# One filler object through the recurrence and the attention, its first weights split earlier, the recurrence's preparation cut into parts, and its stores issued by ACT

## The reference

```python
def in_proj(xn, w_in, b_fgate, lb):                 # xn: (1, 2048, 1024); w_in: (1024, 8200)
    h = xn @ w_in
    fq, fk, fv, ff, fz, hq, hf, hi, hz, mq, mz, ga, gb, gm = split(h)
    f = lb + (1.0 - lb) * sigmoid(hf)               # hg_k = 1 - f, hg_logf = log(f)
    ...
def fox_prompt(q, k, v, logf):                      # 8 heads x 64, causal
    sc = q @ k.T * scale + c[:, None] - c[None, :]  # c = cumsum(logf)
    return softmax(sc) @ v
def hgrn2(q, k, v, logf, s0, chunk):                # 4 heads x 128, over chunks of rows
    b = cumsum(logf)
    o = (q . exp(b[t] - b[s]) . k) @ v + (q * exp(b)) @ S
    S = exp(b[-1]) * S + (k * exp(b[-1] - b)).T @ v
def merge_branches(...):
    mixed = sigmoid(ga) * ya + sigmoid(gb) * yb + sigmoid(gm) * ym
    return x + mixed @ w_o
```

## Time and profile before

| | us |
|---|---|
| median of 3 runs | 3652.9 |
| lowest and highest | 3644.84 and 3656.94 |
| profiled execution | 3645.66 |
| its span, first to last instruction | 3644.1 |
| TensorE busy in it | 2951.2 (81%) |
| DVE, ACT, POOL busy | 1490.2, 954.3, 581.9 |
| mean granted TensorE clock | 0.899 |

### The profile page before, as it was taken

The page is one execution under the profiler, slowest core; times in us unless marked ns, Lnnn a source line. Parts: engine busy times, 40 slices in busy tenths (PEclk is TensorE's granted clock), DMA queues, the critical chain, the costliest instruction groups (busy, mean ns, idle before and its releaser), DMA issues. The chain is left out here.

```text
span 3644.1 us, 38245 instructions
## 1 busy us (share of the span) xinstructions
PE 2951.2 (81%) x13930; PEld 2335.6 (64%) x13930; DVE 1490.2 (41%) x2774; ACT 954.3 (26%) x1806; POOL 581.9 (16%) x539
## 2 busy tenths in 40 slices
PE   4969999999239777868499999999922386799999
PEld 3847777887127565657377787778822232588887
DVE  3510001111345454553455555555556622544444
ACT  1201111111023232222244454444400110423222
POOL 2021111110252324140201002020035300000000
PEclk8979999999559898989799999999966698899999
DMA  3325422211446454534555545554366476533331
GB/s 133 104 63 160 144 67 70 70 67 51 162 152 199 150 169 144 186 121 155 168 151 148 157 130 151 150 157 138 100 211 203 129 220 193 189 114 115 120 120 47
DMA packets 304488, 499.36 MB, mean 137 GB/s; under 512 B 109028, under 2 KB 150535, under 8 KB 285607
## 3 DMA queue, kind: packets, MB, share of 16 engines
q1 hardware_dynamic: 298399, 479.43, 41.9%
q0 software_dynamic: 5904, 17.51, 1.6%
HBM read 386.18 MB, written 110.67 MB: 136 GB/s over the span
## 5 line engine op out<-in xcount | busy, mean ns | idle before, releaser
L2246 PE MATMUL hgfill_out<-hgfill_w_hi,hgfill_x 128*128 128x512 f32 x1024 | 360.4, 429 | 77.4 <-DMA hgfill_x<-x_tiles 50.9
L2246 PE MATMUL fill_out<-fill_w_hi,fill_x 128*128 128x512 f32 x1024 | 374.4, 418 | 0.0
L477 DVE TENSOR_TENSOR in_stage<-in_stage,in_out 128x512 f32<-128x512 f32 x64 | 44.0, 687 | 624.3 <-ACT in_stage L466 624.3
L2246 PEld LDWEIGHTS hgfill_out<-hgfill_w_hi,hgfill_x 128*128 128x128 f32 x1024 | 204.3, 205 | 128.2 <-issue 53.5
L823 DVE TENSOR_TENSOR fox_pt_lo<-fox_turned,fox_pt_hi 128x512 fp32r<-128x512 f32 (+1 forms) x320 | 194.9, 609 | 191.5 <-ACT fox_pt_hi L773 189.9
L773 ACT ACTIVATE fox_pt_hi<-fox_turned 128x512 fp32r<-128x512 f32 (+1 forms) x320 | 170.4, 533 | 361.2 <-PE fox_turned L728 360.6
L809 DVE CUSTOM_DVE_ANT_0 fox_probs<-fox_scores,fox_bias 128x512 f32<-128x512 f32 (+2 forms) x320 | 187.8, 609 | 108.3 <-PE fox_scores L717 66.9
L179 PE MATMUL in_out<-x_hi,in_whi 128*128 128x512 f32 x512 | 205.9, 402 | 19.8 <-POOL in_wlo L421 19.8
L466 ACT ACTIVATE in_stage<-in_out 128x512 f32<-128x512 f32 x112 | 67.0, 599 | 588.0 <-PE in_out L181 588.0
L2246 PE MATMUL hgfill_out<-hgfill_w_lo,hgfill_x 128*128 128x512 f32 x512 | 217.5, 425 | 0.0
L2246 PE MATMUL fill_out<-fill_w_lo,fill_x 128*128 128x512 f32 x512 | 212.2, 414 | 0.0
(11 more groups left out here) (374 smaller groups left out, 6141.4 us busy)
## 6 DMA issues: line engine op xcount, KB each, us to landing
hgfill_x<-x_tiles SPq DMA_DIRECT2D x64, 1024.0 KB, 5.5
fill_x<-x_tiles SPq DMA_DIRECT2D x64, 1024.0 KB, 5.4
paged_slot<-in_cache_fox_k_dram SPq DMA_DIRECT2D x128, 256.0 KB, 3.0
paged_slot<-in_cache_fox_v_dram SPq DMA_DIRECT2D x128, 256.0 KB, 3.0
mf_gate<-plain SPq DMA_DIRECT2D x96, 256.0 KB
turned<-in_stage SPq DMA_DIRECT2D x64, 256.0 KB
plain<-fill_stage SPq DMA_DIRECT2D x64, 256.0 KB, 5.4
in_raw<-in_w_in_dram SPq DMA_DIRECT2D x56, 256.0 KB, 3.1
```

Source lines behind the costliest of these rows:

```text
L477: dve.tensor_tensor(stage[u % STAGES][:], stage[u % STAGES][:], out[u % STAGES][:], ALU.mult).then_inc(taken, 1)
L2246: ins = pe.matmul(self.out[n % self.OUTS][:], x, w, start=(k == 0 and term == 0), stop=(ends and term == 2))
```

## The change

There is one `Filler`, `fill`, for all eight groups and 3200 matmuls. It is made ahead of `unpack_sample`; each stage calls `begin` with the number of matmuls for each of its slots (`spread`).

- In `unpack_sample` SP loads the first two x tiles and the single rows (`sync_start`), POOL loads and splits the first group's eight slices (`gpsimd_start`, `gpsimd_first`). The work of `lower_bound` moves into this block too, and its own block is gone. SP's stores of zeros stand last.
- In `recur_prompt` the preparation is in four parts. Iteration n does part (n + 5) mod 4 of unit (n + 5) div 4; iterations -5 to -1 have no chunk, only parts and fillers. 1600 fillers lie in 138 slots. ACT's copy of a filler unit may stand between `rows_of_keys` and `take`. SP stores a piece of gated rows two iterations after the chunk in which DVE makes it, and loads q and f of a later unit at a unit's first chunk instead of its last.
- In `attend_prompt` nine `fill` steps stand among the first `set`, `keys`, `score` and `exp` (100 matmuls), and 1500 in the 160 key steps. POOL no longer splits a first group there: that of the fifth group is done by the recurrence's last slots.
- ACT waits for its own copy out of PSUM and issues the store of that unit itself. SP only loads x tiles.

```diff
-    steps = [("set", 0)] + [("keys", 0, b) for b in range(QUADS)]
+    steps = [("fill", 0), ("set", 0)]
+    for b in range(QUADS):
+        steps += [("fill", 1 + b), ("keys", 0, b)]
     for i in range(4):
-        steps += [("score", 0, i, 0), ("exp", 0, i)]
+        steps += [("score", 0, i, 0), ("fill", 1 + QUADS + i), ("exp", 0, i)]
+    FILLS = 1 + QUADS + 4
...
+    PARTS, AHEAD = 4, 5
+
     def walk(prepare, early, late, post, extra):
 
-        for n, (blk, h, c) in enumerate(chunks):
-            if n == 0:
-                prepare(0)
-            if c == 0 and n // CH + 1 < len(units):
-                prepare(n // CH + 1)
-            early(n)
-            if n > 0:
+        for n in range(-AHEAD, len(chunks)):
+            if n >= 0:
+                early(n)
+            if n >= 1:
                 late(n - 1)
-            if blk > 0 and n % BLOCK in POST_AT:
-                post(blk - 1, POST_AT.index(n % BLOCK))
+            if n >= BLOCK and n % BLOCK in POST_AT:
+                post(n // BLOCK - 1, POST_AT.index(n % BLOCK))
+            u, part = divmod(n + AHEAD, PARTS)
+            if u < len(units):
+                prepare(u, part)
             extra(n)
...
+        fill.begin(fill.spread(matmuls, 2 * (len(chunks) + AHEAD)))
...
-                    if c == CH - 1 and n // CH + HH < len(units):
+                    if n >= 0 and n % CH == 0 and n // CH + HH < len(units):
                         load_unit(n // CH + HH)
...
+                    if n >= BLOCK and n % BLOCK - 2 in POST_AT:
+                        store(n // BLOCK - 1, POST_AT.index(n % BLOCK - 2))
...
+                def prepare(u, part):
                     blk, h = units[u]
+                    if part == 1:
+                        differences(u, h)
+                    if part != 0:
+                        return
...
+                    if part == 0:
+                        act.wait_ge(f_ready, u + 1)
+                        act.activation(log_f[:], f[h][:], ACT.Ln).then_inc(log_ready, 1)
...
+                def early(n):
+                    rows_of_keys(n)
+                    fill.scalar(act, slots_of(n)[0])
...
+                fill.sync_start(sp)
...
+                fill.gpsimd_start(pool)
                 pool.memset(zeros[:], 0.0).then_inc(cleared, 1)
+                fill.gpsimd_first(pool)
...
         act.activation(self.stage[n % self.STAGES][0:rows, :], self.out[n % self.OUTS][0:rows, :], ACT.Copy
                        ).then_inc(self.taken, 1)
+        act.wait_ge(self.taken, n + 1)
+        self.store(act, n)
...
-        sp.wait_ge(self.taken, n + 1)
-        sp.dma_start(self.sample[group.sample] if self.is_sample(n) else group.place(u),
+        act.dma_start(self.sample[group.sample] if self.is_sample(n) else group.place(u),
...
+MATMULS = {"recur": 1600, "first": 100, "fox": 1500}
```

More of the change, by code:

```diff
@@ L653, in _ @@
                     load_bias(0)
-                    fill.sync_start(sp)
                     for n in range(2):
@@ L1009, in _ @@
                     load_z(n)
-                walk(lambda u: None, lambda n: None, lambda n: None, post, extra)
+                walk(nothing, nothing, nothing, nothing, extra)
+                for piece in range(PIECES):
+                    store(BLOCKS - 1, piece)
                 sp.wait_ge(state_ready, len(chunks))
@@ new lines, in prepare @@
+                    if part == 0:
+                        dve.wait_ge(log_ready, u + 1)
+                        for c in range(CH):
+                            at = slice(c * P, (c + 1) * P)
+                            last = dve.tensor_tensor_scan(b[h][:, at], ones[:], log_f[:, at], 0.0, ALU.mult, ALU.add)
+                        last.then_inc(b_ready, 1)
+                    if part == 1:
+                        dve.wait_ge(k_ready, u + 1)
+                        dve.wait_ge(exp_ready, u * ES + 1)
+                        dve.tensor_tensor(q_run[h][:], q_run[h][:], q[h][:], ALU.mult)
@@ L1220, in _, with extra @@
                 pe.wait_ge(consts, 1)
-                walk(lambda u: None, pairs, sums, lambda blk, piece: None, lambda n: fill.tensor(pe, 2 * n + 1))
+                def extra(n):
+                    if n < 0:
+                        fill.tensor(pe, slots_of(n)[0])
+                    fill.tensor(pe, slots_of(n)[1])
+                walk(nothing, pairs, sums, nothing, extra)
 def attend_memory(nc, core, queries, mem_k, mem_v, z_mem, gated, cache):
@@ L2203, in matmuls_of, with begin, spread, left @@
         return (len(group.tiles) - 1) * 3 * KT + KT * (5 if group.sample is not None else 3)
+    def begin(self, counts):
+        base = self.edges[-1]
+        self.edges = [base + sum(counts[:n]) for n in range(len(counts) + 1)]
+        self.slots = len(counts)
+        assert self.edges[-1] <= self.total
+    @staticmethod
+    def spread(matmuls, slots):
+        return [matmuls * (n + 1) // slots - matmuls * n // slots for n in range(slots)]
+    def left(self):
+        return self.total - self.edges[-1]
     def until(self, slot):
-        return self.total * min(slot, self.slots) // self.slots
+        return self.edges[slot]
     def group_of(self, counts, n):
```

268 lines of the change are left out of this document (131 added, 137 removed).

## The result

| | median us (runs) | ratio to the kernel before, 95% interval |
|---|---|---|
| before, same chip | 3649.1 (4) | 1 |
| changed | 3508.8 (4) | 0.9613 [0.9584, 0.9641] |

The change gains 140 us, 3.9%. The forecast was 3520 (3470 to 3590). The profiled execution has a span of 3514.1 us, that of before 3644.1, so 130.0 less. Where they lie I read from five places that both kernels have: POOL's first instruction of a block, DVE's last product of `hg_state`, SP's first load of `fox_k_raw` and TensorE's last filler on an x tile with `w_hi`.

What follows compares the result with a forecast made beforehand. Blocks run one by one; TensorE fills the attention, while the recurrence is held by something serial. Recurrence -121, unpacking +19.5, lower bound -4.65, attention -23.5 sum to -129.7 from 3645.66, so 3516; forecast 3520 us, range 3470 to 3590.

Steps and rivals of the forecast that it cites:

- What bounds the kernel: Whole program: blocks run one after another; attention is TensorE's own, the recurrence (busy 531.00 of 673.00 us) has something serial.
- Recurrence, 577 forecast: Recurrence up to its window's end: 577.4 us against 698.7 before, a gain of 121 us.
- undisturbed work: Recurrence: with nothing holding TensorE a chunk takes 7.67 us, 25 fillers included; all 64 chunks take 491 us.
- splits: Recurrence: TensorE's waits for split weights at three changes of group rise from 26.4 to 38 us: 16, 14.5 and 7.6.
- x tiles: Recurrence: SP's stores of gated rows stand two chunks later and block nothing; 4 of 50.9 us of waits remain.
- DVE late: Recurrence: DVE's normalisation piece delays the level products; weights come some 2 us late, 2.3 with signals, three times: 7 us.
- The waits for `hg_k_rows` go: Recurrence: with preparation in four parts and ACT's copies between them, all 60.0 us of these waits go.
- The tail stays: Behind the recurrence: the tail of 19 us stays; POOL's split for the attention's first group is hidden in it.
- Unpacking +19.5: Unpacking block: splitting the first weights on POOL adds 19.5 us on the path, bounds 16 and 26.
- Attention -23.5: Attention: 100 fillers moved ahead save 23 us, the clock 4.5; ACT's stores cost 4; gain 23.5 us.
- ACT's stores, 4 us in the attention: Attention: each unit costs ACT 0.5 to 1.0 us, nearly all hidden; 4 us taken, bounds 0 and 68.
- The signs named ahead: Profile after: early fillers, `hg_k_rows` waits gone, x tiles below 10 us, splits about 38, clock over 0.92, next block near 935.

## Why the prediction was right, and where its terms were not

**What bounds the kernel**: confirmed. Blocks were read one by one, and the recurrence was the one with room.

**Recurrence, 577 forecast, 533 measured.** By terms, forecast and measured: constants 7.6 and 7.6; undisturbed work 491 and 473; low clock 28.5 and 18; splits 38 and 28.4; x tiles 4 and 3.7; DVE late 7 and 0; waits for ACT's copies none and 2.1. The 473 are 64 chunks at 6.97 us (most are 6.92 apart, some 7.15) and 5 lead chunks of 23.2 fillers, 0.23 each. The 18 is TensorE's busy time of 491.31 less that; it is a remainder that no row gives by itself, so it is no check that the measured terms add up to 533. The term that was too dear is the 7.67 us a chunk. Its unit held a wait that I did not subtract. These are the unit's stretch in the trace of before, at a granted clock of 1.00, so without slow matmuls, and the row of its first chunk:

```profile
1329.00:1361.20 32.20, 30.04 (x161) 25.43 (x162) 18.46 (x27) 12.18 (x28) 7.91 (x8) 1.00 0.67 212
```

```profile
1332.74 0.46 PE L1212 MATMUL hg_o_sum<-hg_v,hg_weights 128*128 128x128 f32 x2 [0.65 <-DVE hg_state L1161]
```

That chunk takes 8.38 us, the next two 7.38, the last 7.54 without the 1.51 that I subtracted. I took the lengthening of one unit for the pace of all 16. Chunks between waits in the trace of before are 7.38 us apart, and 64 of them are 472. At the start I took 15 us of low clock; fillers were 0.23 us apart from 1069.7 on, 4.7 us behind the first, so 2.4 us lost and not 7.5.

**The waits for `hg_k_rows` go**: right, and the run in one piece shows that cutting it is what does it, 54 of the 164 us. What comes late otherwise is whatever ACT holds behind the unit, not this tile alone.

**x tiles**: the number was right (4 and 3.7), the cause half wrong. The later store of gated rows alone does nothing (3507.3); with SP's stores of units it counts some 12 to 19 us where the preparation is in one piece, and where it is in parts 12 in the trace and nothing in the medians. Of 33.7 of the 50.9 us the cause stays open.

**Splits**: POOL's order was read rightly. At the first change the differences stand ahead of the last two slices, and the whole takes from 1170.33 to 1202.99, 32.7 us for the 31 forecast:

```profile
1191.87 0.55 POOL L2366 DMA_DIRECT2D fill_raw<-in_w_in_dram  x1 [0.30 <-POOL fill_w_lo L2382]
1192.43 3.09 POOL L1022 TENSOR_TENSOR hg_level<-hg_b 128x512 f32<-128x512 f32 x3
...
1198.22 0.60 POOL L2380 CAST fill_w_hi<-fill_raw 128x512 fp32r<-128x512 f32 x1
```

The three changes cost 11.9, 10.9 and 5.6 us of waits where I had 16, 14.5 and 7.6. What was short is TensorE's own work up to the last slice: 32.7 - 11.9 = 21 us, and 30.6 - 10.9 = 20 at the second change, not 15.

**DVE 2 us late, three times**: it did not happen. The products are at 417 ns. The Trainium skill (SBUF — State Buffer, "SBUF: two separate sides") says that DVE and GpSimd share a port pair that one of them holds for a whole instruction while the other waits; by it I had 7 us less and did not take them. The traces agree: 417 ns at the median where POOL is idle during 44 of the 48, 1293 where it works during 44.

**The tail stays**: off by 5. POOL did end ahead of DVE as I said, so I called it hidden. But its slices stretched six of DVE's steps from 1.2 to as much as 2.3 us, 4.1 us together; 0.8 is a wait for ACT's last copy of `hg_o_rows`. Work that is hidden in time still took from the engine that set the end.

**Unpacking +19.5**: 23.2, within 16 to 26. POOL ended at 943.4, 28.7 us in and not 27, and the next block opened 3.6 us behind it and not 1. It is on the path: 11 to 15 us came back when the splits were moved.

**Attention -23.5**: the step that failed. I removed 100 fillers from a stage that TensorE fills and took their time off. Four of the nine first steps stand behind the first score, so 45 of the 100 stayed in the main stage, and 55 x 0.23 = 13 us were freed. The keys took 9.4 of these (17 us of waits became 26.4), and the waits for `fox_probs` rose from 2.4 to 5.1 us; with SP's stores they are 1.5, so that rise comes with ACT's. TensorE's own rows behind the first score fell by 9.5 us (820.7 to 811.3) and not by 13, and the 4.5 us that I gave for the clock don't show. So this stretch is 1.6 us longer, and the one ahead of the first score, which I left, 2.3 shorter. That keys bound the place was in the earlier trace rows only for the start; the 17 us behind it I had not counted as a limit.

**ACT's stores, 4 us in the attention**: of the right size, if they cost anything. Four kernels with them have 892.7 us on average, three with SP's 889.9, and the lowest of the four is below the highest of the three; with the keys first it is 854.0 and 847.2, in two kernels that differ in the place of the split too. So 0 to 7 us, and nothing is gained. The Trainium skill (DMA: Bandwidth & Descriptors, "Issuing engines are not separate DMA queues") has it so, and the runs agree: 3499.6 with SP's stores, 3508.8 with ACT's.

**The signs named ahead**: fillers within 8 us, no wait for `hg_k_rows`, x tiles below 10 us, the clock over 0.92, ACT waited for less than 10 us in the attention (5.1, 1.9 and less) all came. The waits for splits rose by 2 us and not by 12. TensorE was busy 22.83 of 36 us ahead of the first quad, where I wanted over 30 of 41. The block behind the unpacking opened at 947, 7.8 of it because this run was late already.

The errors were +43 in the recurrence, and on the other side 22.8 in the attention, 5 in the tail, 3.7 and 1.5 in the blocks ahead, 1.7 at the end and 7.8 of chance ahead of the change. They cancel, so that the total came out right is luck; the parts were not right.

## What to carry to other kernels

Cut a serial chain over several engines into parts and let the small copies stand between them; what it frees is everything queued behind it, not only the tile in the list of waits. Before you take work off the stage that looks full, list what its bound engine still waits for: it may hand most of the gain to a load that is queued behind another not needed for 100 us. Look at each load on a queue for what it is needed by, and put the one that is needed last last: that alone gave 32 to 38 us, where the move of stores to another engine gave none.

## What the runs showed of the hardware

- A DVE product of 128x256 takes 417 ns alone and 1293 ns beside POOL's differences; one of 128x1024 1.22 us alone and up to 2.29 beside POOL's slices. A reduction of 128x1024, which has one input, takes 1.22 us beside the same slices too (at 1602.65 in the changed kernel, while POOL works on `fill_w_lo` from 1601.62 to 1603.74).
- An issue on SP's queue, 0.33 us at the median for an x tile and 0.51 for keys, took 4.99 us for an x tile behind loads of queries and values, and 6.3 us for one of keys; the loads behind it wait as long.
- ACT's issue of a store is 0.33 to 0.34 us at the median, less than POOL's 0.55 of a load of the same size.
